# Sixteen modulation blocks as narrow products on TensorE, with the first group's loads, row squares and scales in another order

## The chip, the cores and the metric

The kernel runs on one core of a Trainium2 chip. The metric is the device time of one execution in microseconds; three runs of the kernel before took 1738.68, 1740.67 and 1740.92 us, median 1740.67. TensorE does the matrix products, VectorE (DVE) and ScalarE (ACT) the elementwise work, GpSimd (POOL) a few elementwise operations, and SyncE (SP) issues nearly all loads.

## The reference, cut to what matters

Two transformer blocks on 256 tokens of width 1024, in float32. The change touches only the start of the first block, where a condition vector makes shift and gain for a normalised input that is then projected:

```python
mod = silu(c) @ w_mod + b_mod               # 6 x 1024; and the same with c_ctx
h  = rms_norm(x,   norm1_g) * (1 + mod[1])   + mod[0]
hc = rms_norm(ctx, norm1_g) * (1 + mod_c[1]) + mod_c[0]
proj, projc = h @ w_in, hc @ w_in            # then retention and attention heads
# attention, w_out, PEER experts (16384), then a second block: FFN, gated MLP, SSM, FFN, gate
```

## The kernel before, in words

All large weights come from one array, `wall`, in chunks of 1024 KB (128 x 2048 float32), each made of two halves. They land in three buffers, `raw`. SP issues the load of chunk n when both halves of chunk n-3 have been read (`read(u)`, L548). A half of a projection weight is read by two operations: ACT rounds it to `w_hi` (L1410), and DVE or POOL writes the rest as `w_lo` (L1851 or L2602); TensorE then makes three products per tile from the pairs. Up to four such pairs are held, made ahead of use in the order that `REACH` sets.

The first ten chunks hold the 16 blocks of `w_mod` for shift (blocks 0 to 7) and gain (8 to 15), each 1024 x 128, and the four halves `win 0,0` to `win 0,3` of the first projection group. A "quarter" h is the four blocks 2h, 2h+1, 2h+8, 2h+9, which give shift and gain of the feature blocks 2h and 2h+1 for x and for ctx. One list, `front_steps` (L150), is walked by every engine, and each does its part of each step in that order:

- `mod n`: for n below 8, DVE multiplies the 128 x 1024 block by the condition row of ctx (L2010) and of x (L2013), each with a sum along the row. For n in `MOD_PE` (8 to 15) TensorE does it: eight products (sixteen in the trace, which shows a float32 product with few columns as two) with the block as the stationary operand and only two moving columns, c and c_ctx (`mod_block`, L888). These are the narrow products. From block 16 on, DVE does them with its own loads.
- `diag 0`, `diag 1`: scale of the rows of x and of ctx as diagonal matrices, from row squares made by ACT.
- `xturn h`, `cturn h`: TensorE transposes and scales two feature blocks of x, of ctx ("turns"). A turn waits until the one before it in the same bank has been read (`s_f`, `s_fh`).
- `gain h` (`gains`, L2019): DVE adds the bias and makes the gain from the four blocks of a quarter. `rows h`: DVE and ACT scale, shift and split the turned blocks into `HX` (x) and `HC` (ctx).
- `win 0,h`: TensorE's 12 products of 512 columns over `HX`. It waits for the two `HX` blocks of rows h and for the `w_lo` half.
- `evac 0`: ACT copies the finished projection out of the banks, which lets the next group (`win 1,0`) start. Behind it stand the squares and roots of `unit 0` and `unit 1`, with block 16 of `w_mod` between them.

Of the kernel before, what the change touches and what calls it, by code (L numbers as in the profile page):

```python
# [142 lines left out]

MOD_PE = list(range(8, 16))
NMOD = 16


def front_steps():  # L150


    steps = []

    def mods(*ns):
        steps.extend(("mod", n) for n in ns)

    def win(p, h, *more):
        steps.append(("win", p, h))
        steps.extend(more)  # L160

    mods(0, 8, 1, 9)
    steps.extend([("diag", 0), ("xturn", 0)])
    mods(2)
    steps.extend([("diag", 1), ("cturn", 0), ("gain", 0), ("rows", 0)])
    mods(10, 3, 11)
    steps.extend([("xturn", 1), ("cturn", 1), ("gain", 1), ("rows", 1)])
    win(0, 0)
    mods(12, 4, 13, 5)
    steps.extend([("xturn", 2), ("cturn", 2), ("gain", 2), ("rows", 2)])  # L170
    win(0, 1)
    mods(14, 6, 15, 7)
    steps.extend([("xturn", 3), ("cturn", 3), ("gain", 3), ("rows", 3)])
    win(0, 2)
    win(0, 3, ("evac", 0))
    win(1, 0, ("square", 0), ("square", 1), ("unit", 0))
    mods(16)
    win(1, 1, ("rope", 0), ("unit", 1))
    mods(17, 18)
    win(1, 2, ("rope", 1))  # L180
    mods(19, 20)
    win(1, 3, ("evac", 1), ("gammas", 0))
    mods(21)
    win(2, 0, ("square", 2), ("square", 3), ("unit", 2), ("qturn", 0), ("qturn", 1))
    mods(22)
    win(2, 1, ("rope", 2), ("unit", 3), ("qturn", 2), ("qturn", 3))
# [12 lines left out]
    steps.extend([("score", 2), ("weigh", 0), ("turn", 1)])
    win(4, 0, ("score", 3), ("weigh", 1), ("turn", 2))  # L200
    mods(30, 31)
    steps.extend([("score", 4), ("weigh", 2), ("turn", 3)])
    win(4, 1, ("score", 5), ("weigh", 3), ("turn", 4), ("rope", 4))
    mods(32, 33)
    win(4, 2, ("score", 6), ("weigh", 4), ("turn", 5), ("rope", 5))
    mods(34, 35)
    win(4, 3, ("evac", 4), ("score", 7), ("weigh", 5), ("turn", 6))
    mods(36, 37)
    mods(38, 39)
    steps.extend([("weigh", 6), ("turn", 7), ("rturn", 0)])  # L210
    win(5, 0, ("mask", 0), ("weigh", 7))
    win(5, 1, ("rturn", 1), ("mask", 1), ("madd", 0))
    win(5, 2, ("rscore", 0), ("mask", 2), ("dvar", 0), ("madd", 1))
    win(5, 3, ("added", 1), ("droot", 0), ("rscore", 1), ("evac", 5), ("madd", 2), ("dnorm", 0))
    steps.extend([("rweigh", 0), ("rscore", 2), ("mask", 3), ("rweigh", 1), ("dblocks", 0), ("madd", 3)])
    steps.extend([("out", 0), ("rscore", 3), ("out", 1), ("rweigh", 2), ("rweigh", 3), ("rnorm", 0)])
    steps.extend([("out", 2), ("out", 3)])
    return steps
# [7 lines left out]

SPLIT = [u for u in range(U_END) if u >= U_OUT1 or HALVES[u][0] == "win"]
ORD = {u: n for n, u in enumerate(SPLIT)}
LO_POOL |= {HALF_OF["win", p, h] for p in (0,) for h in range(4)}

GATE2 = range(40, 48)
MOD_V = [s[1] for s in FRONT if s[0] == "mod" and s[1] not in MOD_PE] + list(GATE2)
# [152 lines left out]
def program(nc, wall, keys_d, cols_d, rows_d, bigrows_d, crow_d, wmod_d, dist_d, x_d, ctx_d, pT_d, gws_d, out_d, n_chunks):  # L385
    assert n_chunks * 2 == U_END
    with ExitStack() as es:
# [413 lines left out]

        def sync_program(e):
            e.dma_start(cols[:, :], cols_d).then_inc(s_tab, 16)
            e.dma_start(crow_ctx, crow_d[1024:2048].partition_broadcast(128)).then_inc(s_crow, 16)
            e.dma_start(crow, crow_d[0:1024].partition_broadcast(128)).then_inc(s_crow, 16)
            for n in range(n_chunks):
                if n == 1:
                    e.dma_start(x[:, :, :], x_d.rearrange("(i p) d -> p i d", p=128)).then_inc(s_x, 16)
                if n == 2:
                    e.dma_start(ctx, ctx_d.rearrange("(i p) d -> p i d", p=128)).then_inc(s_ctx, 16)  # L810
                if n == 6:
                    e.dma_start(rows[:, :], rows_d.partition_broadcast(128)).then_inc(s_tab, 16)
                if n == 10:
                    e.wait_ge(s_tab, 32)
                    e.dma_start(dist, dist_d.rearrange("p (a b) -> p a b", a=4)).then_inc(s_tab, 16)
                if n == 11:
                    e.wait_ge(s_c2, 3)
                    e.dma_start(crow_keep.rearrange("(p d) -> p d", p=1), crow[0:1, :]).then_inc(s_ckeep, 16)
                if n == U_QUERY // 2:
                    e.wait_ge(s_pt_, 8)  # L820
# [7 lines left out]
                for m in MOD_ISSUE.get(n, []):  # L828
                    place, times = mod_slot(m)
                    if m < NMOD + 4:  # L830
                        e.wait_ge(*summed(7))
                        e.wait_ge(s_std, 2)
                    elif m == GATE2[0]:
                        e.wait_ge(s_w, 24)
                        e.wait_ge(s_ckeep, 16)
                        e.dma_start(crow2, crow_keep.partition_broadcast(128)).then_inc(s_rawm[4], 16)
                    else:
                        e.wait_ge(*summed(m - (1 if m in GATE2 else 4)))
                    e.dma_start(mod_raw[place], wmod_d[m - NMOD]).then_inc(s_rawm[place], 16)
# [26 lines left out]
        def tensor_program(e):  # L866
# [23 lines left out]
            def mod_block(n):  # L890
# [1 line left out]
                w = raw_half(u).rearrange("p (k n) -> p k n", k=8)  # L892
                t.wait_ge(*landed(u))
                t.wait_ge(s_c2, 1)
                quarter, q = n % 8 // 2, MOD_PE.index(n)
                if quarter >= 2:
                    t.wait_ge(s_mod, quarter - 1)
                for k in range(8):
# [501 lines left out]
        def scalar_program(e):  # L1400
# [109 lines left out]

            a.wait_ge(s_tab, 16)
            act(c2, c2, ACT.Silu, sig=s_c2)
            a.wait_ge(s_crow, 32)
            for r in (crow_ctx, crow):
                act(r, r, ACT.Silu, sig=s_c2)
            a.wait_ge(s_set, 1)
            for j, (src, here) in enumerate(((x, s_x), (ctx, s_ctx))):
                a.wait_ge(here, 16)
                for i in range(2):
                    act(scr, src[:, i, :], ACT.Square, scale=1.0 / 32, acc=rs[:, 2 * j + i:2 * j + i + 1])  # L1520
# [3 lines left out]
                return pj(n, 1536, 2048) if n < 2 else pj(n - 2, 2048, 2560)  # L1524

            for name, n, *more in FRONT:
                if name == "gammas":
                    softplus_parts(0, sa[:, 0:8], sb_[:, 0:8], sc[:, 0:8])
                    a.wait_ge(s_lam, 1)
                    act(sa[:, 0:2], sa[:, 0:2], ACT.Exp, sig=s_lama)  # L1530
                elif name == "rows":
                    for b in range(4 * n, 4 * n + 4):
                        high(b)
                    ahead(HALF_OF["win", 0, n], only=True)
                elif name == "win":
                    ahead(HALF_OF[(name, n, *more)])
                elif name == "evac":
                    g, u = GROUPS[n], HALF_OF["win", n, 3]
                    for i in tiles_of(g):
# [4 lines left out]
                            a.wait_ge(s_win, WIN_MADE[n, i])  # L1544
                        src = PB[2][:, 256 * (i == 2):256 + 256 * (i == 2)] if narrow else PB[i][:, :]
                        act(pj(i, g * 512 + 256 * narrow, (g + 1) * 512), src, ACT.Silu if g == 2 else ACT.Copy, sig=s_wev)
                elif name == "square":
                    if n >= 2:
                        a.wait_ge(s_qn, n - 1)
# [294 lines left out]
        def vector_program(e):  # L1844
# [29 lines left out]
                v.settle()  # L1874
                v.did(e.reciprocal(out, a_), sig)

            def ahead(u):

                nonlocal made
                while made < REACH[u]:  # L1880
                    w = SPLIT[made]
                    if w not in LO_POOL:
                        v.wait_ge(s_hi, made + 1)
# [111 lines left out]
            def mod_block(n):  # L1995


                c_ = crow
                if n >= NMOD:
                    place, times = mod_slot(n)  # L2000
                    w = mod_raw[place]
                    if n >= GATE2[0]:
                        times, c_ = times + 1, crow2
                    v.wait_ge(s_rawm[place], 16 * times + 16)
                else:
                    u = HALF_OF["mod", n]
                    w = raw_half(u)
                    v.wait_ge(*landed(u))
                    v.wait_ge(s_c2, 2)
                    v.did(e.scalar_tensor_tensor(junk, w, 1.0, crow_ctx, MUL, MUL, accum_out=modT[:, n, 1:2]))  # L2010
                    v.wait_ge(s_c2, 3)
                v.settle()
                v.did(e.scalar_tensor_tensor(w, w, 1.0, c_, MUL, MUL, accum_out=modT[:, n, 0:1]), s_modv)  # L2013

# [3 lines left out]

            def gains(h):  # L2019

                quarter = (2 * h, 2 * h + 1, 2 * h + 8, 2 * h + 9)
                v.wait_ge(s_modu, max(MOD_PE.index(n) for n in quarter if n in MOD_PE) + 1)
                for n in quarter:
                    src = modT[:, n, :]
                    if n in MOD_PE:
                        src = pm[h % 2][:, MOD_PE.index(n), :]
                    ts(modT[:, n, :], src, col("bmod")[:, n:n + 1], op0=ADD, sig=s_mod if n == 2 * h + 9 else None)
                s_ = slice(2 * h, 2 * h + 2)
                stt(G1[:, s_, :], modT[:, 2 * h + 8:2 * h + 10, :], 1.0, bc(col("n1")[:, s_], 2, 2), ADD, MUL)

# [57 lines left out]
            for name, n, *more in FRONT:  # L2088
# [21 lines left out]
                elif name == "rows":  # L2110
                    scaled(4 * n)
                    scaled(4 * n + 1)
                    for b in range(4 * n, 4 * n + 4):
                        low(b)
                elif name == "win" and (n, *more) != (5, 3):
                    ahead(HALF_OF[(name, n, *more)])
# [637 lines left out]
```

## Time and profile before

| | |
|---|---|
| median of three runs | 1740.67 us |
| profiled execution: span from the first to the last instruction | 1738.2 us |
| lowest and highest run | 1738.68 and 1740.92 us |
| PE, DVE, ACT busy | 1647.9, 1250.9, 907.9 us |
| the front, up to the first product of `win 1,0` | 71.38 us |

The profile gives the profiled execution its span; the time of that execution as a whole is not given apart from the three runs, whose lowest lies 0.5 us and whose median 2.5 us above the span. TensorE is busy 95% of the span, but in the front it is not: the change touches the first 4% of the span alone. A chain of waits is read from the end backwards; the timeline of an engine gives its groups of instructions in order of time, with the idle time before a group in brackets and what ended it. `ar` is the large work area (it holds ctx, the condition rows, the attention arrays), `pb` the accumulation banks, `raw` the chunks.

### The profile page before, as it was taken

The page shows a single profiled execution, that of the slowest core. Times are in us where ns is not written, and L with a number is a line of the kernel's source. Part 1 is how long each engine was busy: PE and PEld are TensorE (multiplying, and loading weights), DVE is VectorE, ACT ScalarE, POOL GpSimd, SP SyncE. Part 2 cuts the span into 40 slices and gives each one's busy share as a digit, 9 for nine tenths or more (in the row PEclk, how much of TensorE's full clock was granted, in tenths as well). Part 3 has the DMA queues.
Part 4 walks back from the last instruction along what each step waited for, and adds up shares of the span by engine and source line. Part 5 has one row for each costly group of instructions (what it writes and reads, how often), then busy time and mean ns, then how long its engine had stood idle before and what let it go on. Part 6 is the DMA issues. An engine that isn't in the chain of part 4 may idle for free.

```text
span 1738.2 us, 29000 instructions
## 1 busy us (share of the span) xinstructions
PE 1647.9 (95%) x11512; PEld 1479.5 (85%) x11512; DVE 1250.9 (72%) x2028; ACT 907.9 (52%) x1192; POOL 83.8 (5%) x50
## 2 busy tenths in 40 slices
PE   6898788999999999999999999999998989999997
PEld 6776668998999888789999999899998777899996
DVE  5886666899988899986666655655557787655556
ACT  4354555554555555455444445544446766644446
POOL 1100003522000000000000000000000000000000
PEclk9898999999999999999999999999999999999999
DMA  6644233446565455566555565454554533555551
GB/s 264 274 168 157 97 118 137 155 161 206 189 202 188 170 207 192 207 218 249 203 211 216 195 214 187 150 204 177 194 173 155 203 137 121 200 194 174 193 191 73
DMA packets 53418, 318.52 MB, mean 183 GB/s; under 512 B 5953, under 2 KB 6113, under 8 KB 19362
## 3 DMA queue, kind: packets, MB, share of 16 engines
q1 hardware_dynamic: 52098, 310.60, 50.2%
q0 software_dynamic: 1184, 6.05, 0.9%
q8 instruction: 91, 1.49, 0.3%
q14 instruction: 45, 0.37, 0.1%
HBM read 307.17 MB, written 9.47 MB: 182 GB/s over the span
## 4 chain that ended last, share of the span: by engine, by line
PE 73%; DVE 18%; ACT 6%; issue 1%; DMA 1%; SPq 0%; DVEq 0%; ACTq 0%
PE pb L870 73%; DVE w_lo L1851 4%; DVE ar L1851 4%; ACT ar L1410 3%; DVE ar L1863 2%; ACT w_hi L1410 2%; DVE ar L2215 1%; DMA raw<-in_wall 1%; DVE ar L2013 1%; DVE ar L2212 1%; DVE raw L2013 1%; ACT L1410 1%; DVE ar L2010 1%; DVE ar L2219 1%; DVE sm L2078 0%
## 5 line engine op out<-in xcount | busy, mean ns | idle before, releaser
L1851 DVE TENSOR_TENSOR w_lo<-raw,w_hi 128x1024 fp32r<-128x1024 f32 x467 | 572.2, 1225 | 253.2 <-ACT w_hi L1410 227.7
L870 PE MATMUL pb<-HX,w_hi 128*128 128x256 f32 x3904 | 715.8, 285 | 13.0 <-DVE w_lo L1851 6.0
L1410 ACT ACTIVATE w_hi<-raw 128x1024 fp32r<-128x1024 f32 x498 | 528.3, 1061 | 299.3 <-PE pb L870 278.3
L870 PEld LDWEIGHTS pb<-HX,w_hi 128*128 128x128 f32 x3904 | 613.8, 193 | 20.1 <-DVE w_lo L1851 5.2
L870 PE MATMUL pb<-HX,w_lo 128*128 128x256 f32 x1952 | 553.7, 284 | 0.0
L870 PE MATMUL pb<-w_hi,HC 128*128 128x512 f32 (+1 forms) x1648 | 526.3, 391 | 4.2 <-DVE HC L1863 3.3
L870 PEld LDWEIGHTS pb<-HX,w_lo 128*128 128x128 f32 x1952 | 376.0, 193 | 0.0
L870 PEld LDWEIGHTS pb<-w_hi,HC 128*128 128x128 f32 x1648 | 309.6, 188 | 68.6 <-DVE HC L1863 2.7
L870 PE MATMUL pb<-w_lo,HC 128*128 128x512 f32 (+1 forms) x824 | 320.6, 389 | 0.0
L1851 DVE TENSOR_TENSOR ar<-ar 128x512 bf16<-128x512 bf16 (+8 forms) x470 | 247.7, 564 | 53.2 <-ACT ar L1410 33.5
L1410 ACT ACTIVATE ar<-pb 128x512 f32<-128x512 f32 (+3 forms) x200 | 112.4, 562 | 256.5 <-PE pb L870 155.4
L870 PE MATMUL pb<-w_hi,HX 128*128 128x512 f32 x512 | 175.2, 409 | 10.6 <-DVE HX L1851 4.2
L870 PEld LDWEIGHTS pb<-w_lo,HC 128*128 128x128 f32 x824 | 155.3, 188 | 28.9
L870 PE MATMUL pb<-ar 128*128 128x64 bf16 (+3 forms) x1960 | 127.9, 224 | 19.1 <-ACT ar L1410 8.8
L870 PEld LDWEIGHTS pb<-ar 128*128 128x128 bf16 (+2 forms) x1960 | 106.5, 121 | 42.4 <-issue 22.6
L870 PEld LDWEIGHTS pb<-w_hi,HX 128*128 128x128 f32 x512 | 99.7, 195 | 36.9 <-issue 7.9
L1410 ACT ACTIVATE HC<-ar 128x512 fp32r<-128x512 f32 x87 | 55.0, 633 | 93.4 <-PE pb L870 52.1
L870 PE MATMUL pb<-w_lo,HX 128*128 128x512 f32 x256 | 102.3, 400 | 0.0
L1851 DVE TENSOR_TENSOR HC<-ar,HC 128x512 fp32r<-128x512 f32 x87 | 60.3, 693 | 45.0 <-ACT HC L1410 41.3
L2602 POOL TENSOR_TENSOR w_lo<-raw,w_hi 128x1024 fp32r<-128x1024 f32 x31 | 75.8, 2444 | 151.1 <-ACT w_hi L1410 110.9
L1410 ACT ACTIVATE ar<-ar 128x512 f32<-128x512 f32 (+6 forms) x85 | 50.2, 591 | 52.5 <-DVE ar L1858 18.0
L870 PEld LDWEIGHTS pb<-w_lo,HX 128*128 128x128 f32 x256 | 50.1, 196 | 9.2
(148 smaller groups left out, 705.5 us busy)
## 6 DMA issues: line engine op xcount, KB each, us to landing
raw<-in_wall SPq DMA_DIRECT2D x257, 1024.0 KB, 4.8
ar<-in_wmod SPq DMA_DIRECT2D x24, 512.0 KB, 3.7
act_keep<-ar SPq DMA_DIRECT2D x28, 256.0 KB, 5.6
ar<-act_keep SPq DMA_DIRECT2D x28, 256.0 KB, 5.1
x<-in_wmod SPq DMA_DIRECT2D x8, 512.0 KB, 5.3
ar<-in_bigrows POOLq DMA_DIRECT2D x2, 1024.0 KB, 5.3
ar<-acs_keep POOLq DMA_DIRECT2D x2, 1024.0 KB, 8.2
ar<-in_crow SPq DMA_DIRECT2D x2, 512.0 KB, 6.0
```

Source lines behind the costliest of these rows:

```text
L870: return e.matmul(o, l, r, start=start, stop=stop, skip_group_check=True)
L1410: a.did(e.activation(out, in_, func, scale=scale, **kw), sig)
L1851: v.did(e.tensor_tensor(out, a_, b_, op), sig)
L1863: v.did(e.scalar_tensor_tensor(out, a_, s_, b_, op0, op1), sig)
L2010: v.did(e.scalar_tensor_tensor(junk, w, 1.0, crow_ctx, MUL, MUL, accum_out=modT[:, n, 1:2]))
L2013: v.did(e.scalar_tensor_tensor(w, w, 1.0, c_, MUL, MUL, accum_out=modT[:, n, 0:1]), s_modv)
L2212: v.did(e.max(vals[:, c_], src))
L2215: v.did(e.max_index(idx[:, c_], vals[:, c_], src))
L2219: v.did(e.match_replace(src, vals[:, c_], src, NEG))
L2602: p.did(e.tensor_tensor(w_lo[:, made % NH, :], raw_half(w), w_hi[:, made % NH, :].bitcast(F32), SUB), s_lop)
```

## The change

`MOD_PE` holds all sixteen blocks, ordered by quarters. DVE no longer does a block below 16. The whole of quarter 0 now stands ahead of `diag 0`, and `cturn h` stands behind `gain h`; `xturn h+1` stands ahead of `win 0,h`. The row squares move into the step `diag`. The broadcast load of the ctx condition row is gone and that of c (512 KB) moves from the head of the queue to chunk 8; its silu moves behind `evac 0`. The bias of a quarter is added by one operation in place of four. The `w_lo` halves of `win 0,0` to `win 0,3` go from POOL to DVE, and in `rows h` the `win 0,h` half stands ahead of the two ctx blocks.

```diff
-MOD_PE = list(range(8, 16))
+MOD_PE = [0, 8, 1, 9, 2, 10, 3, 11, 4, 12, 5, 13, 6, 14, 7, 15]
...
-    mods(0, 8, 1, 9)
+    def quarter(h):
+        mods(*MOD_PE[4 * h:4 * h + 4])
+
+    quarter(0)
     steps.extend([("diag", 0), ("xturn", 0)])
-    mods(2)
-    steps.extend([("diag", 1), ("cturn", 0), ("gain", 0), ("rows", 0)])
-    mods(10, 3, 11)
-    steps.extend([("xturn", 1), ("cturn", 1), ("gain", 1), ("rows", 1)])
+    quarter(1)
+    steps.extend([("gain", 0), ("diag", 1), ("cturn", 0), ("rows", 0), ("xturn", 1)])
     win(0, 0)
...
+    quarter(3)
+    steps.extend([("gain", 2), ("cturn", 2), ("rows", 2), ("xturn", 3)])
     win(0, 2)
+    steps.extend([("gain", 3), ("cturn", 3), ("rows", 3)])
     win(0, 3, ("evac", 0))
...
-LO_POOL |= {HALF_OF["win", p, h] for p in (0,) for h in range(4)}
...
-            e.dma_start(crow_ctx, crow_d[1024:2048].partition_broadcast(128)).then_inc(s_crow, 16)
-            e.dma_start(crow, crow_d[0:1024].partition_broadcast(128)).then_inc(s_crow, 16)
...
+                if n == 8:
+                    e.dma_start(crow, crow_d[0:1024].partition_broadcast(128)).then_inc(s_crow, 16)
...
                 elif name == "rows":
-                    for b in range(4 * n, 4 * n + 4):
+                    for b in (4 * n, 4 * n + 1):
                         high(b)
                     ahead(HALF_OF["win", 0, n], only=True)
+                    for b in (4 * n + 2, 4 * n + 3):
+                        high(b)
...
+                    if n == 0:
+                        a.wait_ge(s_crow, 16)
+                        act(crow, crow, ACT.Silu, sig=s_c2)
...
-                for n in quarter:
-                    src = modT[:, n, :]
-                    if n in MOD_PE:
-                        src = pm[h % 2][:, MOD_PE.index(n), :]
-                    ts(modT[:, n, :], src, col("bmod")[:, n:n + 1], op0=ADD, sig=s_mod if n == 2 * h + 9 else None)
+                v.wait_ge(s_modu, 4 * h + 4)
+                pair = slice(2 * h, 2 * h + 2)
+                tt(modT[:, 0:16, :].rearrange("p (s k) j -> p s k j", s=2)[:, :, pair, :],
+                   pm[h % 2][:, h // 2 * 4:h // 2 * 4 + 4, :].rearrange("p (s k) j -> p s k j", s=2),
+                   bc(col("bmod")[:, 0:16].rearrange("p (s k) -> p s k", s=2)[:, :, pair], 3, 2), ADD, sig=s_mod)
```

The start of TensorE's program before: `cols,raw` are narrow products (eight to a block), `ar,x` is a turn of x, `ar` alone a turn of ctx, `w_hi,HX` and `w_lo,HX` a projection half.

```order
L870 MATMUL pb<-cols,raw 128x2 x16
L870 MATMUL pb<-ar,x 128x128 x4
L870 MATMUL pb<-ar 128x128 x4
L870 MATMUL pb<-cols,raw 128x2 x16
L870 MATMUL pb<-ar,x 128x128 x4
L870 MATMUL pb<-ar 128x128 x4
L870 MATMUL pb<-w_hi,HX 128x512
```

The same place with the change:

```order
L870 MATMUL pb<-cols,raw 128x2 x32
L870 MATMUL pb<-ar,x 128x128 x4
L870 MATMUL pb<-cols,raw 128x2 x32
L870 MATMUL pb<-ar 128x128 x4
L870 MATMUL pb<-ar,x 128x128 x4
L870 MATMUL pb<-w_hi,HX 128x512
```

Two blocks between turns have become four, in every quarter; the first two quarters stand ahead of `win 0,0` with one turn between them.

DVE's program from the scaling of rows 2 to that of rows 3, before (`fsc<-pb` and `HX` are the x blocks, `HC` the ctx blocks, L2010 and L2013 the row products of a block of `w_mod`, `modT` and `sm` the gain):

```order
L1858 TENSOR_SCALAR fsc<-pb,sm,modT 128x256 x2
L1851 TENSOR_TENSOR HX<-fsc,HX 128x256 x2
L1851 TENSOR_TENSOR HC<-fsc,HC 128x256 x2
L2010 SCALAR_TENSOR_TENSOR ar,modT<-raw,ar 128x1024
L2013 SCALAR_TENSOR_TENSOR raw,modT<-raw,ar 128x1024
L2010 SCALAR_TENSOR_TENSOR ar,modT<-raw,ar 128x1024
L2013 SCALAR_TENSOR_TENSOR raw,modT<-raw,ar 128x1024
L1856 TENSOR_SCALAR modT<-modT,cols 128x2 x2
L1856 TENSOR_SCALAR modT<-pb,cols 128x2 x2
L1863 SCALAR_TENSOR_TENSOR sm<-modT,cols 128x4
L1858 TENSOR_SCALAR fsc<-pb,sm,modT 128x256 x2
```

The same place with the change:

```order
L1863 TENSOR_SCALAR fsc<-pb,sm,modT 128x256 x2
L1856 TENSOR_TENSOR HX<-fsc,HX 128x256 x2
L1856 TENSOR_TENSOR HC<-fsc,HC 128x256 x2
L1856 TENSOR_TENSOR w_lo<-raw,w_hi 128x1024 x2
L1856 TENSOR_TENSOR modT<-pb,cols 128x2x4
L1868 SCALAR_TENSOR_TENSOR sm<-modT,cols 128x4
L1863 TENSOR_SCALAR fsc<-pb,sm,modT 128x256 x2
```

The four row products are gone from between the two, and two `w_lo` halves of group 1 have come from behind rows 3 to ahead of `gain 3`.

ACT's program around `evac 0` (`ar<-pb` copies the banks out, `ar<-ar 128x1024` is the silu of the condition row, `ar<-ar 128x512` the squares, `ar<-ar 128x8` the root), as a difference:

```order
+L1410 ACTIVATE w_hi<-raw 128x1024
 L1410 ACTIVATE ar<-pb 128x512 x2
+L1410 ACT_TABLE_LOAD
+L1410 ACTIVATE ar<-ar 128x1024
 L1410 ACTIVATE w_hi<-raw 128x1024
 L1410 ACTIVATE ar<-ar 128x512 x2
+L1410 ACT_TABLE_LOAD
 L1410 ACTIVATE ar<-ar 128x8
```

A silu with its table, and the table of the root again, now stand between the copies out of the banks and the root of `unit 0`.

## Rows read from the trace of the kernel before

**Rows 1.** The chain of waits, 0 to 160 us: start, us, what.
```profile
57.26 3.32 DVE ar L2010 x2
...
71.38 22.07 PE pb L870 x96
```
**Rows 2.** Groups by line, 0 to 71.3 us: busy, mean ns, idle before.
```profile
L870 PE MATMUL pb<-cols,raw 128*128 128x2 f32 x128 | 21.2, 300 | 12.1 <-DMA raw<-in_wall 12.1
L2013 DVE SCALAR_TENSOR_TENSOR raw<-raw,ar 128x1024 f32<-128x1024 f32 x8 | 15.9, 1982 | 0.3
...
L2010 DVE SCALAR_TENSOR_TENSOR ar<-raw,ar 128x1024 f32<-128x1024 f32 x8 | 11.9, 1490 | 14.7 <-DMA raw<-in_wall 14.7
```
**Rows 3.** Timeline of PE in the front: start, us, idle before.
```profile
10.65 3.58 PE L870 MATMUL pb<-cols,raw 128*128 128x2 f32 x16 [10.65 <-DMA raw<-in_wall]
15.69 3.58 PE L870 MATMUL pb<-cols,raw 128*128 128x2 f32 x16 [1.47 <-DMA raw<-in_wall]
...
26.10 6.83 PE L870 MATMUL pb<-cols,raw 128*128 128x2 f32 x32
32.79 2.05 PE L870 MATMUL pb<-ar,x 128*128 128x128 f32 x8
...
36.20 0.70 PE L870 MATMUL pb<-w_hi,HX 128*128 128x512 f32 x1
...
39.27 3.63 PE L870 MATMUL pb<-cols,raw 128*128 128x2 f32 x32
42.76 1.39 PE L870 MATMUL pb<-ar,x 128*128 128x128 f32 x8
...
45.51 0.77 PE L870 MATMUL pb<-w_hi,HX 128*128 128x512 f32 x1
...
48.99 3.63 PE L870 MATMUL pb<-cols,raw 128*128 128x2 f32 x32
52.47 1.14 PE L870 MATMUL pb<-ar,x 128*128 128x128 f32 x8
...
65.42 0.77 PE L870 MATMUL pb<-w_hi,HX 128*128 128x512 f32 x1 [4.17 <-DVE HX L1851]
...
70.25 0.63 PE L870 MATMUL pb<-w_hi,HX 128*128 128x512 f32 x1
```
**Rows 4.** Stretches of 1 us; the column after POOL is the granted clock.
```profile
43.00:44.00 1.00, 1.00 (x9) 1.00 (x9) 1.00 (x1) 0.00 (x0) 0.23 (x1) 0.75 0.92 385
...
53.00:54.00 1.00, 1.00 (x10) 1.00 (x9) 0.97 (x2) 0.97 (x2) 0.40 (x1) 0.87 0.42 164
```
**Rows 5.** Timeline of ACT at the start and around `evac 0`.
```profile
4.04 0.22 ACT L1410 ACTIVATE cols<-cols 128x16 f32<-128x16 f32 x1 [1.96 <-DMA cols<-in_cols]
...
64.93 0.56 ACT L1410 ACTIVATE fsc<-pb,modT,sm 128x256 f32<-128x256 f32 x1
...
67.17 3.38 ACT L1410 ACTIVATE w_hi<-raw 128x1024 fp32r<-128x1024 f32 x3
70.64 1.29 ACT L1410 ACTIVATE ar<-pb 128x512 f32<-128x512 f32 x2
...
94.15 1.28 ACT L1410 ACT_TABLE_LOAD   x1
```
**Rows 6.** Timeline of DVE in and behind the front.
```profile
63.25 1.12 DVE L1858 TENSOR_SCALAR fsc<-pb,sm,modT 128x256 f32<-128x256 f32 x2
...
74.41 0.69 DVE L1871 TENSOR_REDUCE ar<-ar 128x8 f32<-128x512 f32 x1
...
95.69 0.17 DVE L1856 TENSOR_SCALAR sm<-sm 128x8 f32<-128x8 f32 x1 [0.71 <-ACT sm L1410]
97.27 0.38 DVE L1856 TENSOR_SCALAR sm<-sm 128x8 f32<-128x8 f32 x2 [1.41 <-ACT sm L1410]
```
**Rows 7.** Loads, 0 to 110 us: KB each, median us from issue to landing.
```profile
raw<-in_wall SPq DMA_DIRECT2D x17, 1024.0 KB, 5.6
```
**Rows 8.** The page's group of the `w_lo` halves on DVE.
```profile
L1851 DVE TENSOR_TENSOR w_lo<-raw,w_hi 128x1024 fp32r<-128x1024 f32 x467 | 572.2, 1225 | 253.2 <-ACT w_hi L1410 227.7
```

More of the change, by code:

```diff
@@ L160, in win @@
         steps.extend(more)
-    mods(0, 8, 1, 9)
+    def quarter(h):
+        mods(*MOD_PE[4 * h:4 * h + 4])
+    quarter(0)
     steps.extend([("diag", 0), ("xturn", 0)])
-    mods(2)
-    steps.extend([("diag", 1), ("cturn", 0), ("gain", 0), ("rows", 0)])
-    mods(10, 3, 11)
-    steps.extend([("xturn", 1), ("cturn", 1), ("gain", 1), ("rows", 1)])
+    quarter(1)
+    steps.extend([("gain", 0), ("diag", 1), ("cturn", 0), ("rows", 0), ("xturn", 1)])
     win(0, 0)
-    mods(12, 4, 13, 5)
-    steps.extend([("xturn", 2), ("cturn", 2), ("gain", 2), ("rows", 2)])
+    quarter(2)
+    steps.extend([("gain", 1), ("cturn", 1), ("rows", 1), ("xturn", 2)])
     win(0, 1)
-    mods(14, 6, 15, 7)
-    steps.extend([("xturn", 3), ("cturn", 3), ("gain", 3), ("rows", 3)])
+    quarter(3)
+    steps.extend([("gain", 2), ("cturn", 2), ("rows", 2), ("xturn", 3)])
     win(0, 2)
+    steps.extend([("gain", 3), ("cturn", 3), ("rows", 3)])
     win(0, 3, ("evac", 0))
@@ L569, in program @@
         assert a2.at <= 2048
-        crow_ctx, scr, junk = msk[:, 0, :], msk[:, 1, :], msk[:, 2, :]
+        scr = msk[:, 1, :]
         def pj(i, a, b):
@@ L808, in sync_program @@
                     e.dma_start(x[:, :, :], x_d.rearrange("(i p) d -> p i d", p=128)).then_inc(s_x, 16)
-                if n == 2:
+                if n == 3:
                     e.dma_start(ctx, ctx_d.rearrange("(i p) d -> p i d", p=128)).then_inc(s_ctx, 16)
-                if n == 6:
+                if n == 8:
+                    e.dma_start(crow, crow_d[0:1024].partition_broadcast(128)).then_inc(s_crow, 16)
+                if n == 9:
                     e.dma_start(rows[:, :], rows_d.partition_broadcast(128)).then_inc(s_tab, 16)
@@ L815, in sync_program @@
                     e.dma_start(dist, dist_d.rearrange("p (a b) -> p a b", a=4)).then_inc(s_tab, 16)
-                if n == 11:
-                    e.wait_ge(s_c2, 3)
+                if n == U_OUT1 // 2 - 1:
+                    e.wait_ge(s_c2, 2)
                     e.dma_start(crow_keep.rearrange("(p d) -> p d", p=1), crow[0:1, :]).then_inc(s_ckeep, 16)
@@ L830, in sync_program @@
                     if m < NMOD + 4:
-                        e.wait_ge(*summed(7))
                         e.wait_ge(s_std, 2)
@@ L894, in mod_block @@
                 t.wait_ge(s_c2, 1)
-                quarter, q = n % 8 // 2, MOD_PE.index(n)
+                quarter, q = n % 8 // 2, 4 * (n % 8 // 4) + n // 8 * 2 + n % 2
                 if quarter >= 2:
@@ L1512, in scalar_program, with row_squares @@
             act(c2, c2, ACT.Silu, sig=s_c2)
-            a.wait_ge(s_crow, 32)
-            for r in (crow_ctx, crow):
-                act(r, r, ACT.Silu, sig=s_c2)
             a.wait_ge(s_set, 1)
-            for j, (src, here) in enumerate(((x, s_x), (ctx, s_ctx))):
+            def row_squares(j, src, here):
                 a.wait_ge(here, 16)
@@ L1526, in scalar_program @@
             for name, n, *more in FRONT:
-                if name == "gammas":
+                if name == "diag":
+                    row_squares(n, *((ctx, s_ctx) if n else (x, s_x)))
+                elif name == "gammas":
                     softplus_parts(0, sa[:, 0:8], sb_[:, 0:8], sc[:, 0:8])
@@ L1875, in rcp, with ahead @@
                 v.did(e.reciprocal(out, a_), sig)
-            def ahead(u):
+            def ahead(u, only=False):
                 nonlocal made
-                while made < REACH[u]:
+                while made < (ORD[u] + 1 if only else REACH[u]):
                     w = SPLIT[made]
@@ L1998, in mod_block @@
                 c_ = crow
[L1999 to L2004, printed above, removed]
-                else:
-                    u = HALF_OF["mod", n]
-                    w = raw_half(u)
-                    v.wait_ge(*landed(u))
+                place, times = mod_slot(n)
+                w = mod_raw[place]
+                if n >= GATE2[0]:
+                    times, c_ = times + 1, crow2
+                else:
                     v.wait_ge(s_c2, 2)
-                    v.did(e.scalar_tensor_tensor(junk, w, 1.0, crow_ctx, MUL, MUL, accum_out=modT[:, n, 1:2]))
-                    v.wait_ge(s_c2, 3)
+                v.wait_ge(s_rawm[place], 16 * times + 16)
                 v.settle()
@@ L2019, in gains @@
             def gains(h):
-                quarter = (2 * h, 2 * h + 1, 2 * h + 8, 2 * h + 9)
-                v.wait_ge(s_modu, max(MOD_PE.index(n) for n in quarter if n in MOD_PE) + 1)
-                for n in quarter:
-                    src = modT[:, n, :]
-                    if n in MOD_PE:
-                        src = pm[h % 2][:, MOD_PE.index(n), :]
-                    ts(modT[:, n, :], src, col("bmod")[:, n:n + 1], op0=ADD, sig=s_mod if n == 2 * h + 9 else None)
+                v.wait_ge(s_modu, 4 * h + 4)
[3 more added lines that the diff above has]
+                   bc(col("bmod")[:, 0:16].rearrange("p (s k) -> p s k", s=2)[:, :, pair], 3, 2), ADD, sig=s_mod)
                 s_ = slice(2 * h, 2 * h + 2)
@@ L2112, in vector_program @@
                     scaled(4 * n + 1)
-                    for b in range(4 * n, 4 * n + 4):
+                    for b in (4 * n, 4 * n + 1):
+                        low(b)
+                    ahead(HALF_OF["win", 0, n], only=True)
+                    for b in (4 * n + 2, 4 * n + 3):
                         low(b)
```

## The prediction, as made before the changed kernel ran

> **What bounds the kernel now.** I read the chain of waits first, then the groups of the first 71 us, then the timelines of TensorE, ScalarE and VectorE. The reader is to see in the chain that the front hangs on the row products of `w_mod` blocks on VectorE and the small operations that follow them, and from 71.38 us TensorE with 22 us of projection without a break [rows 1]. Before them stand the first loads, for which TensorE waits 12.1 us [rows 2]. In the groups, the 16 row products on VectorE take 15.9 + 11.9 = 27.8 us (means 1.98 and 1.49 us). TensorE's eight narrow blocks take 21.2 us [rows 2]. So VectorE is the bound of the front and TensorE has gaps, the last 4.17 us before `win 0,3` [rows 3]. Everything behind 71.38 us hangs on that point: no load or engine runs to a clock of its own. The effect of the change is the shift of that restart, plus what is new just behind it.
>
> **TensorE's two speeds.** This decides. The same two narrow blocks take 6.83 us at 26.10 and 3.63 at 39.27 [rows 3]. The granted clock reads 1.00 over the first 43 us, so there I go by durations; from 43 us both agree: it falls to half (1.2 GHz) at about 43.5 and 53.7 from 2.4 GHz [rows 4]. Start to start, a block costs (32.79 - 26.10)/2 = 3.35 us at the low clock, 3.54 from 15.69; I take 3.4. At the high clock (42.76 - 39.27)/2 = 1.75. A turn costs (36.20 - 32.79)/2 = 1.7 low and at most 1.14 high (at 52.47) [rows 3]; I take 1.0. What comes before each change is regular: with narrow products alone the clock never rose, though TensorE worked on them from 26.10 to 32.79; turns and a projection half raised it. It fell 43.5 - 39.27 = 4.2 us and 53.7 - 48.99 = 4.7 us after a row of narrow products had begun, each time when they were already over, so the two blocks were still fast and the turns behind them slow.
>
> **The change part by part, along TensorE.**
>
> *Start.* The two condition loads of 512 KB leave the head of the queue. `cols` is there at 4.04 and the first chunk at 10.65 [rows 3, 5]: 6.6 us for 2048 KB, of which 1024 remain: 3.3 us, so the first chunk lands at 7.35 (bounds 6.5, at the pace of 5.0 us for x and a chunk, 10.65 to 15.69, and 8.5).
>
> *Quarter 0.* Four blocks at 3.4 = 13.6: done at 20.95. Chunk 1 (two loads behind the first, 5.0 us) is there at 12.4 and is not waited for. Row squares and scales of x are done by then, since ctx and x come no later than before.
>
> *Turn 0, quarter 1.* 1.7, then 13.6 at the low clock: 36.25. Chunk 3 is asked for when chunk 0 has been read, at 14.2, and comes behind the queue at about 20; it is needed at 29.5. Later chunks take 5.6 us from the request [rows 7], and each request comes a quarter or more ahead of its use. Loads bound nothing from 7.35 on.
>
> *Turns and `win 0,0`.* Two turns 3.4: 39.65. The clock rises about here, as it did before `win 0,0`, which takes 39.27 - 36.20 = 3.07 [rows 3]: 42.7. Its `HX` blocks and its half are ready 15 us earlier.
>
> *Quarter 2.* Four blocks from the high clock. It falls some 4.5 us after they begin: 4.5/1.75 = 2.6 blocks fast, 1.4 slow at 3.4 = 4.8. Together 9.3: 52.0.
>
> *Turns, `win 0,1`, quarter 3, turns, `win 0,2`.* 3.4 (slow), 48.99 - 45.51 = 3.5, 9.3, 3.4, 3.5: 75.1. The last turn at the high clock, 1.0: 76.1.
>
> *`win 0,3`.* Its `HX` blocks are now late for a new reason. ctx turn 2 ends at 71.6 - 1.7 = 69.9. Then ACT makes the ctx blocks of rows 2, 67.17 - 64.93 = 2.2 [rows 5]: 72.1; then two `w_hi` halves at 3.38/3 = 1.13: 74.4; VectorE's second `w_lo`, which stands ahead of `gain 3`, 1.2 [rows 8]: 75.6; gain 0.4 (an estimate: two small operations in place of five); scaling and splitting the two x blocks 65.42 - 63.25 = 2.2 [rows 3, 6]: 78.2. TensorE waits 2.1 us in place of 4.17. With 3.0 for the half it ends at 81.2, and by the lead of before (the first half of group 1 begins when ACT has copied a bank out, 71.38 [rows 1] against a `win 0,3` that ends at 70.9 [rows 3]) group 1 begins at 81.6 (ACT itself, with 2.2 for the ctx blocks and 1.1 for one more `w_hi`, gets there no later). Against 71.38: **+10.2 us**.
>
> *Behind `evac 0`.* A table load 1.28 [rows 5] and a silu of 128 x 1024, which has the shape of a `w_hi` at 1.1 [rows 5], stand ahead of the squares: VectorE's `unit 0` is 2.4 us later. The second table load lies in VectorE's reduction but for 0.3. VectorE then works nearly without a break to 95 us, where it waits 0.71 and 1.41 us for ACT [rows 6]; the first of these swallows 0.7, the second recurs, as it is ACT's own table change. **+1.9 us** (bounds 0, if VectorE is not what the later chain hangs on, and 3.7, all three operations in full).
>
> *Nothing.* VectorE's 27.8 us [rows 2] go from the path, but VectorE would then wait for TensorE; its four `w_lo` halves and the three bias additions less per quarter lie under TensorE's quarters. The condition row is needed by block 16 at the earliest and lands 30 us before.
>
> *Sum.* 10.2 + 1.9 = 12.1 us. On the profiled span 1738.2: 1750.3. The median of the runs lies 2.5 us above that span, so the forecast is 1740.7 + 12.1 = **1752.8 us**, 0.7% slower. The trade in one line: TensorE takes eight blocks more, 8 x 1.75 = 14 us at best and 8 x 3.4 = 27 at worst, plus slower turns, and has only 3.3 us of earlier start and the gaps of before to put them in.
>
> **A rule of the Trainium skill.** With narrow products only, from 26.10 to 32.79 and from 10.65 on, the rate stayed at the low clock [rows 3]. The page "TensorE: Matmul & The Clock Gate", section "Why this matters for your kernels", says that TensorE should be kept busy continuously to come to the full clock. By that rule the unbroken quarters 0 and 1 would raise it; the trace here does not agree, as the 6.7 us without a break show. What would follow if it did rise is rival C.
>
> **Rivals.**
>
> *A, the low clock throughout the front.* Longer narrow rows never let it up. A half then costs 5.1 (`win 0,3` before, 65.42 to 70.9, shows 5.5). From 39.65: 5.2, 13.6, 3.4, 5.2, 13.6, 3.4, 5.2, 1.7, 5.2 = 96.2; restart 96.7, +25.3, with 1.9: 1768. For it: `win 0,3` ran low from end to end. Against: two turns and a half raised the clock twice, and they still stand in a row.
>
> *B, the high clock stays once it is up.* From 42.7: quarter 7.0, turns 2.0, half 3.1, quarter 7.0: ctx turn 2 ends at 62.8, `HX` 8.3 later at 71.1, half 3.1: restart 74.7, +3.3, with 1.9: 1746. Against: it fell twice in shorter narrow rows [rows 4].
>
> *C, the other side: the clock rises inside quarter 0 or 1.* Unlike before, TensorE has no gap after 12 us. Quarter 1 and all behind at the high clock: 20.95 + 1.0 + 7.0 + 2.0 + 3.1 = 34.1, + 7.0 + 2.0 + 3.1 + 7.0 = 53.2, ctx turn 2 at 54.2, `HX` at 62.5, restart at 66.1: -5.3, with 1.9 it is -3.4: 1737. It decides from a narrow block of 1.75 us before the first turn of ctx; taking VectorE off the path then wins. Against: 26.10 to 32.79.
>
> **How the numbers follow.** Forecast 0.75 (clock as before in its manner, 1746 to 1760 by the bounds of start, clock phase of up to a half, 2.3 us, and the unit term), A 0.08, B 0.10, C 0.07. The range from 1746 to 1764 holds the forecast's cases and half of B, and leaves A and C out. A measurement of this kernel can tell about 0.2%, 3.5 us: faster is the larger part of C, 0.05; the same 0.05, from the rest of C and the low end of B; slower 0.90.
>
> **What would show each step.** First narrow product near 7.35. Quarters 0 and 1 at 13.6 us each. A granted clock of 0.5 over the end of quarters 2 and 3 and the turns behind them, with quarters of 9 to 10 us. A wait of about 2 us on `HX` ahead of `win 0,3`. The first product of group 1 near 81.6. VectorE's first reduction of `unit 0` 6.2 us behind ACT's first copy (74.41 - 70.64 = 3.8 before [rows 5, 6]), and no other stretch changed. Wrong if quarter 1 runs in 7 us, or if TensorE waits for `raw` loads after 12 us.

## The result, and the profile after

| | before | after |
|---|---|---|
| median of the runs (4 each, same chip) | 1739.68 us | 1752.45 us |
| lowest and highest | 1738.25 and 1740.92 | 1750.86 and 1754.91 |
| profiled execution, span | 1738.2 | 1749.1 |
| PE, DVE, ACT busy | 1647.9, 1250.9, 907.9 | 1670.3, 1225.2, 909.2 |
| first product of `win 1,0` | 71.38 | 83.88 |

The ratio is 1.0075, with 95% interval 1.0061 to 1.0089: 12.8 us slower in medians, 10.9 in the two profiled spans (the profiled execution of after is the fastest of its four, 1750.86). The forecast was 1752.8.

The busy times already tell the trade: VectorE works 25.7 us less, TensorE 22.4 us more. The stretch up to the first product of group 1 (`win 1,0`) shows where; that of after ends 0.2 us behind it. Columns: stretch, length, busy time and instructions of PE, PEld, DVE, ACT and POOL, granted clock, DMA share, GB/s. First before, then after.

```profile
0.00:71.40 71.40, 50.51 (x241) 45.67 (x241) 46.93 (x85) 29.35 (x48) 11.17 (x9) 0.88 0.71 277
```
```profile
0.00:84.10 84.10, 73.92 (x369) 71.11 (x370) 22.16 (x45) 27.16 (x46) 0.30 (x5) 0.86 0.66 252
```

TensorE had 21 us of gaps in its front and now has 10, of which 7.46 are the first load. The chain of waits of after (start, us, what) has TensorE alone from 7.46 to 70.8 where that of before had VectorE's row products [rows 1]:

```profile
1.25 6.16 DMA raw<-in_wall
7.46 63.37 PE pb L870 x328
73.08 1.07 ACT w_hi L1410
74.17 1.24 DVE w_lo L1856
75.50 1.24 DVE w_lo L1856
77.30 0.56 DVE fsc L1863
79.48 4.59 PE pb L870 x12
84.09 0.61 ACT ar L1410
```

TensorE's timeline of after (start, us, idle before), to be laid against [rows 3]:

```profile
7.46 13.82 PE L870 MATMUL pb<-cols,raw 128*128 128x2 f32 x64 [7.46 <-DMA raw<-in_wall]
21.14 2.06 PE L870 MATMUL pb<-ar,x 128*128 128x128 f32 x8
22.99 13.65 PE L870 MATMUL pb<-cols,raw 128*128 128x2 f32 x64
36.50 2.06 PE L870 MATMUL pb<-ar 128*128 128x128 f32 x8
...
39.72 0.49 PE L870 MATMUL pb<-w_hi,HX 128*128 128x512 f32 x1
...
42.58 10.22 PE L870 MATMUL pb<-cols,raw 128*128 128x2 f32 x64
52.67 2.06 PE L870 MATMUL pb<-ar 128*128 128x128 f32 x8
...
56.08 0.71 PE L870 MATMUL pb<-w_hi,HX 128*128 128x512 f32 x1
...
59.14 9.76 PE L870 MATMUL pb<-cols,raw 128*128 128x2 f32 x64
...
72.17 0.77 PE L870 MATMUL pb<-w_hi,HX 128*128 128x512 f32 x1
...
75.71 1.05 PE L870 MATMUL pb<-ar 128*128 128x128 f32 x8
79.48 0.47 PE L870 MATMUL pb<-w_hi,HX 128*128 128x512 f32 x1 [2.71 <-DVE HX L1856]
...
83.45 0.82 PE L870 MATMUL pb<-w_hi,HX 128*128 128x512 f32 x2
84.12 0.39 PE L870 MATMUL pb<-w_lo,HX 128*128 128x512 f32 x1
```

The row at 83.45 holds the twelfth and last product of `win 0,3`, which ends at 84.07, and the first of group 1, which starts at 83.88. The 84.09 at the end of the chain is ACT's second copy out of the banks, not TensorE.

Quarters 0 and 1 run at 3.4 us a block from end to end. Quarters 2 and 3 begin fast and end slow. Stretches of 1 us of after give the points (the clock is the number behind POOL's): it falls at 46.3, 3.7 us into quarter 2, and at 63.4, 4.3 us into quarter 3. It falls once more behind the last turn:

```profile
46.00:47.00 1.00, 1.00 (x8) 1.00 (x8) 0.43 (x1) 0.00 (x1) 0.00 (x0) 0.67 0.59 246
...
63.00:64.00 1.00, 1.00 (x8) 1.00 (x9) 0.85 (x3) 0.71 (x2) 0.00 (x0) 0.70 0.40 66
...
80.00:81.00 1.00, 1.00 (x5) 0.81 (x4) 0.43 (x1) 0.88 (x3) 0.00 (x0) 0.73 1.06 430
...
83.00:84.00 1.00, 1.00 (x4) 0.79 (x3) 0.84 (x1) 0.27 (x1) 0.00 (x0) 0.56 0.26 107
```

That last fall, 1 us into `win 0,3` and right behind a wait of 2.71 us, makes this half cost 4.6 us from its start to its end. Behind it, VectorE's first reduction of `unit 0` moved from 74.41 [rows 6] to 89.59, and TensorE's first product behind it (L937) from 128.59 to 143.28. The chains from there, first before, then after:

```profile
128.59 1.78 PE pb L937 x8
130.36 5.11 PE pb L870 x24
135.47 0.45 PE pb L937 x4
...
234.35 13.03 PE pb L870 x64
278.04 54.03 PE pb L870 x440
```
```profile
143.28 1.09 PE pb L937 x8
144.37 4.17 PE pb L870 x24
148.54 0.45 PE pb L937 x4
...
247.47 13.04 PE pb L870 x64
291.24 54.03 PE pb L870 x440
```

The row of 64 products, called "the x64" from here on, serves as a later mark. The shift is 14.7 us at L937 x8, 13.1 in the third row, and then stays: 13.1 at the x64, 13.2 at the x440, 13.3 at 1020 us. What goes in between is clock: the same 32 products took 6.89 us before (granted clock 0.50 from 129 to 132 us) and 5.26 after (1.00 from 144 to 147). Late in the span the shift falls to 12.5 (1316 us) and, where 64 products took 11.79 us before and 10.14 after, to 10.6 (1459 us). The code there is untouched.

### The profile page after: what moved, and what is told of

The parts are those of the page before. It is cut to its first block, busy times and chain, and to the rows that moved or that the text cites. A ratio compares the mean times of both kernels' runs of the same rounds, so it can differ in the third digit from the quotient of the medians.

```text
span 1749.1 us, 29206 instructions
## 1 busy us (share of the span) xinstructions
PE 1670.3 (95%) x11640; PEld 1504.6 (86%) x11640; DVE 1225.2 (70%) x1988; ACT 909.2 (52%) x1193; POOL 73.2 (4%) x46
## 4 chain that ended last, share of the span: by engine, by line
PE 75%; DVE 17%; ACT 6%; issue 1%; DMA 0%; DVEq 0%; ACTq 0%; SPq 0%
PE pb L870 74%; DVE w_lo L1856 4%; DVE ar L1856 4%; ACT ar L1410 3%; DVE ar L1868 2%; ACT w_hi L1410 2%; DVE ar L2012 1%; DVE ar L2215 1%; DVE ar L2212 1%; ACT L1410 1%; DVE ar L2219 1%; DVE sm L2075 0%; ACT HX L1410 0%; DMA raw<-in_wall 0%; DVE ar L1861 0%
## 5 line engine op out<-in xcount | busy, mean ns | idle before, releaser
L1410 ACT ACTIVATE ar<-ar 128x512 f32<-128x512 f32 (+8 forms) x84 | 49.2, 586 | 49.3 <-DVE ar L1863 17.8
L2602 POOL TENSOR_TENSOR w_lo<-raw,w_hi 128x1024 fp32r<-128x1024 f32 x27 | 64.8, 2401 | 104.0 <-ACT w_hi L1410 63.2
```

The source lines that it names most:

```text
L1410: a.did(e.activation(out, in_, func, scale=scale, **kw), sig)
L2602: p.did(e.tensor_tensor(w_lo[:, made % NH, :], raw_half(w), w_hi[:, made % NH, :].bitcast(F32), SUB), s_lop)
```

## The experiments

Two theories of the 12.8 us were open. **T**: TensorE's own narrow work at the low clock is the cost; waits and the silu are small change. **W**: the new order of the elementwise work (the wait on `HX`, the silu, the halves on VectorE) costs most of it, and sixteen narrow blocks as such would pay. `before` ran in each session: medians 1739.59, 1739.06, 1739.41.

**Silu early.** After, with the silu of the condition row in the step `win 0,1`.

```diff
                     ahead(HALF_OF[(name, n, *more)])
+                    if (n, *more) == (0, 1):
+                        a.wait_ge(s_crow, 16)
+                        act(crow, crow, ACT.Silu, sig=s_c2)
...
-                    if n == 0:
-                        a.wait_ge(s_crow, 16)
-                        act(crow, crow, ACT.Silu, sig=s_c2)
```

> The changed kernel with the silu of the condition row moved ahead of evac 0, into ACT's idle stretch behind the halves of win 0,1; nothing else. Theory (the front's length is TensorE's, and the silu with its table stands on the path behind evac 0): TensorE's front unchanged, unit 0's first reduction 2.3 us nearer to ACT's first copy, TensorE's first use of group 2's result (the first product of line 937 after 128 us) 2 us earlier, whole kernel about 2 us shorter than the change, 1750.5. Rival (VectorE is not what the later chain hangs on there): the reduction moves by 2.3 us, the later point and the whole time by 0.3 or less.

Measured: 1750.76 us (1750.27 to 1751.16, 4 runs), ratio to before 1.0068 (1.0051 to 1.0085). L937 comes at 140.69 in place of 143.28, of which 0.3 is an earlier first load, so the term of about 2.3 us is real at this point. But the next 24 products now run at the low clock, 5.75 us for 4.17, and the x64 comes at 247.09 (247.47), no more than the 0.3 of the start earlier. The term does not reach the later stages: the profiled spans are 1749.2 and 1749.1 us. The median is 1.7 us below that of after, near the 2 expected, but the two sets of runs overlap and can't tell it.

**Halves of group 1 later.** After, with the `w_hi` and `w_lo` halves that stood ahead of rows 3 put behind them.

```diff
-                    ahead(HALF_OF[(name, n, *more)])
+                    ahead(HALF_OF[(name, n, *more)], only=(n, *more) == (0, 2))
```

> The changed kernel with the two high and low halves of group 1 made behind rows 3 and no longer ahead of them. Theory (win 0,3 is late since ACT and VectorE first make two halves of group 1): the wait of 2.7 us on HX ahead of win 0,3 goes, win 0,3 runs at the high clock in 2.8 us where it took 4.6, but ACT then has three w_hi to make before it copies the banks out, so group 1 starts only about 1 us earlier (83.0 against 84.1). Rival (the turns and the gain set win 0,3, not the halves): the wait stays above 2 us and group 1 starts where it did or later.

Measured: 1750.67 us (1749.19 to 1751.23, 4 runs), ratio 1.0069 (1.0053 to 1.0086). The wait on `HX` is gone, but one on ACT takes its place, since ACT makes three `w_hi` ahead of its copies. TensorE's timeline of this run:

```profile
81.95 0.77 PE L870 MATMUL pb<-w_hi,HX 128*128 128x512 f32 x1 [3.41 <-ACT ar L1410]
```

`win 0,3` begins without a wait and takes 3.0 us where it took 4.6, at the high clock. Group 1 begins 1.9 us earlier than after's 83.88, 0.5 of it the earlier first load (6.92), and the x64 comes at 245.27, 2.2 earlier. The wait and the slow half behind it account for about 2 of the 12.8 us, not for most of them. This run alone can't say more, since a new wait stands in the place of the old one.

**Dense products beside the narrow ones.** After, with 512-column float32 products into an unused bank: four ahead of the first block and k behind each block of quarters 0 and 1, k = 1 and k = 2.

```diff
+def dense(k):
+    for _ in range(k):
+        mm(PB[0][:, :], ident, cols[:, NCOL - 512:NCOL], True, True)
```

> The changed kernel with extra TensorE work whose results are not used: four products of 512 float32 columns ahead of block 0 while the first chunk is on its way, and one behind each block of quarters 0 and 1. Clock theory (the narrow blocks cost 3.4 us because the clock stays low over them, and dense products raise it): if one dense product per block is enough, the narrow blocks of quarters 0 and 1 take 1.75 us each, and the two quarters with their extra products about 11 us each. If it is not enough they stay at 3.4 and each quarter takes 20 us. Rival (3.4 us is what sixteen weight loads of a cold buffer or loads from HBM beside them cost, whatever the clock): 3.4 us each also where the granted clock is high.

> As warm1 with two dense products behind each block of quarters 0 and 1. Clock theory: the narrow blocks of quarters 0 and 1 take 1.75 us each, each quarter with its eight extra products 14 to 15 us, so the start of win 0,0 stays within 2 us of where it was though TensorE does 20 products more. Rival (the rate of the narrow products has nothing to do with the clock): 3.4 us each and the two quarters together 40 us, win 0,0 13 us later.

Measured (one run each): 1761.21 us with one, 1755.86 with two. With one, the first two blocks of quarter 0 take 1.84 us, the next 2.46 and 3.41, and in quarter 1 1.98, 2.58, 3.41, 3.41. With two, all eight take 1.84. The granted clock goes with it. With one, it reads 1.00 from 11 to 16 us, 0.50 from 18 to 27, 1.00 from 28 to 30 and 0.50 from 32 to 47; with two, it reads 1.00 from 8.5 to 45. TensorE's timeline with two, start and end of that stretch:

```profile
4.49 5.50 PE L870 MATMUL pb<-cols 128*128 128x512 f32 x8 [4.49 <-DMA cols<-in_cols]
9.83 1.84 PE L870 MATMUL pb<-cols,raw 128*128 128x2 f32 x16
11.54 1.96 PE L870 MATMUL pb<-cols 128*128 128x512 f32 x4
...
35.25 1.84 PE L870 MATMUL pb<-cols,raw 128*128 128x2 f32 x16
```

So the 3.4 us are the clock. They are not the stationary side, which is the same in fast and slow blocks, and not the loads: with one dense product the DMA share is 0.98 from 11 to 16 us, beside the fast blocks, and 0.39 from 18 to 27, beside the slow ones. Narrow products do not hold the clock up here; two dense ones behind each block do, and one does not. Twenty dense products more, and `win 0,0` begins at 40.45 us in place of 39.72: up to there they nearly pay for themselves. Behind it they do not: quarter 2 takes 11.33 us from start to start (10.09 in after), group 1 begins at 85.39, and the one run is 3.4 us above after's median.

**Six blocks back on VectorE.** After, with blocks 2 to 7 as row products again (the condition rows loaded at chunk 2, their silus behind x's squares); a second kernel does this with blocks 4 to 7 alone (rows at chunk 4, silus at `gain 0`).

```diff
-MOD_PE = [0, 8, 1, 9, 2, 10, 3, 11, 4, 12, 5, 13, 6, 14, 7, 15]
+MOD_ALL = [0, 8, 1, 9, 2, 10, 3, 11, 4, 12, 5, 13, 6, 14, 7, 15]
+MOD_PE = [n for n in MOD_ALL if n not in [2, 3, 4, 5, 6, 7]]
```

> The changed kernel with blocks 4 to 7 (the shift blocks of quarters 2 and 3) back on VectorE, and both condition rows loaded behind ctx, their silus in ACT's idle stretch of quarter 1. Theory (TensorE is the bound of the front with the change, and VectorE has some 8 us free in each quarter): quarters 2 and 3 take 3.5 us each on TensorE in place of 10, group 1 starts at 67 to 70 us (84.1 with the change, 71.4 before), whole kernel 1737 to 1740, that is 13 us below the change and level with or just below the kernel before. Rival (VectorE's row products become the bound again, as before): group 1 starts at 72 or later and the time is above that of the kernel before.

> As mix12, and blocks 2 and 3 on VectorE too: quarter 0 all on TensorE, the others split in halves as in the kernel before; condition rows loaded behind chunk 1. Theory: quarter 1 takes 7 us on TensorE in place of 13.5, and group 1 starts at 62 to 68 us: 1731 to 1737. Rival (VectorE is the bound from here on, and gets the blocks in front of gain and rows): no earlier than mix12.

Measured: 1751.25 us with four blocks back (1750.65 to 1753.83, 4 runs, ratio 1.0077, 1.0059 to 1.0094) and 1743.18 with six (1741.4 to 1747.25, 10 runs, 1.0025, 1.0015 to 1.0035). Both are slower than before, where 1737 to 1740 and 1731 to 1737 were expected. Quarters 2 and 3 fall to 3.5 us each, as expected, but most of it turns into a wait. Four blocks back, TensorE's timeline:

```profile
55.44 3.63 PE L873 MATMUL pb<-cols,raw 128*128 128x2 f32 x32
...
68.43 2.07 PE L873 MATMUL pb<-ar,x 128*128 128x128 f32 x8 [8.36 <-DVE fsc L1867]
```

and VectorE's at the same place:

```profile
59.10 2.56 DVE L1860 TENSOR_TENSOR w_lo<-raw,w_hi 128x1024 fp32r<-128x1024 f32 x2 [6.28 <-ACT w_hi L1413]
```

VectorE's row products stand behind two `w_lo` halves, and these wait for a `w_hi` whose chunk ACT itself waited 5.7 us for. The group start that I expected at 67 to 70 us came at 81.42: the order of the halves is a second bound that the narrow products had covered. *Both bounds off* below tests this. With six blocks back, quarter 1 falls to 6.7 us, but group 1 begins at 74.43 in place of 62 to 68, behind a wait at the same place:

```profile
60.68 2.08 PE L873 MATMUL pb<-ar,x 128*128 128x128 f32 x8 [7.57 <-DVE fsc L1867]
```

**POOL's halves.** Before, with nothing changed but its four `w_lo` halves, which go from POOL to VectorE.

```diff
-LO_POOL |= {HALF_OF["win", p, h] for p in (0,) for h in range(4)}
```

> The kernel before with one part of the change alone: the w_lo halves of win 0,0 to 0,3 on VectorE in place of POOL. My view (VectorE's row products are slowed while POOL works beside them: 27.8 us for 16, against 19.6 at 1.22 each): VectorE loses the 8 us of slowing and gains four halves at 1.23, so its chain in the front gets 3 us shorter, 1737 us. Rival (the halves stand in the way of the next quarter on VectorE, and the slowing lay beside waits): the same as before or 2 to 5 us longer.

Measured: 1743.79 us (1741.6 to 1745.25, 10 runs), ratio 1.0023 (1.0013 to 1.0032). My view was wrong in sign. The row products beside POOL are indeed faster, all 1.22 to 1.23 us; in before four of sixteen took 3.24 to 3.38, each while POOL worked. One of the four, in VectorE's and POOL's timelines of before:

```profile
29.69 1.22 DVE L2010 SCALAR_TENSOR_TENSOR ar<-raw,ar 128x1024 f32<-128x1024 f32 x1
...
30.95 3.24 DVE L2013 SCALAR_TENSOR_TENSOR raw<-raw,ar 128x1024 f32<-128x1024 f32 x1
```
```profile
30.55 2.57 POOL L2602 TENSOR_TENSOR w_lo<-raw,w_hi 128x1024 fp32r<-128x1024 f32 x1 [29.65 <-ACT w_hi L1410]
```

But VectorE then stands 4.31 us in front of a half whose `w_hi` isn't there, with the row products queued behind it; TensorE waits 4.01 us at 41.47 and 5.23 at 71.98, and group 1 begins at 77.94, 6.6 us late, of which 1.0 is a later first load in this run. The rival written down beside my view (the halves stand in the way of the next quarter, 2 to 5 us longer) is what happened.

**Both bounds off.** Six blocks back on VectorE, and in the front each engine makes only the half of its own quarter in rows h; of group 1, one half ahead of the copies of `evac 0` and the others behind.

```diff
-                while made < (ORD[u] + 1 if only else REACH[u]):
+                while made < (ORD[u] + int(only) if only else REACH[u]):
...
-                    ahead(HALF_OF[(name, n, *more)])
+                    ahead(HALF_OF[(name, n, *more)], only=n == 0)
                 elif name == "evac":
+                    if n == 0:
+                        ahead(HALF_OF["win", 0, 3], only=2)
```

> mix10 with one thing more: in the front each engine makes the halves of win 0,h only in rows h, and those of group 1 only at evac 0 (one ahead of the copies out of the banks, three behind), so that neither ACT nor VectorE stands before a chunk that has not landed while row products and scales could be made. Theory (mix10 lost its gain to that order: VectorE stood 5.3 us for the high half of win 0,2, and TensorE 7.6 us for the scales of x behind it): those two waits fall below 2 us each, group 1 starts at 64 to 68 us, whole kernel 1732 to 1737, faster than the kernel before. Rival (the chunk itself is late, whatever the order: three buffers and 5 to 9 us of landing bound the front): the waits only change their names, group 1 starts at 71 or later, 1740 or more.

Measured: **1735.31 us** (1733.85 to 1737.19, 10 runs), ratio to before 0.998 (0.997 to 0.9989): faster than both kernels, as expected, with group 1 at 65.17 us. No wait of TensorE in the front behind the first load is over 1.5 us:

```profile
7.01 13.81 PE L873 MATMUL pb<-cols,raw 128*128 128x2 f32 x64 [7.01 <-DMA raw<-in_wall]
...
43.52 0.50 PE L873 MATMUL pb<-w_hi,HX 128*128 128x512 f32 x1 [1.50 <-DVE w_lo L1864]
...
51.92 2.08 PE L873 MATMUL pb<-ar,x 128*128 128x128 f32 x8 [0.93 <-DVE fsc L1871]
...
65.17 0.50 PE L873 MATMUL pb<-w_hi,HX 128*128 128x512 f32 x1 [1.21 <-DVE w_lo L1864]
```

Of the 6.2 us by which group 1 begins earlier than in before, 3.6 are the earlier first load (7.01 for 10.65). Against before, this kernel differs in the split, the order of the loads and the order of the halves together; no run tells what each of them is worth.

**All sixteen, with the waits off.** After, with the late halves of the kernel above and the silu early: what is left of the loss when only the narrow products are.

> The changed kernel (all sixteen blocks on TensorE) with the same late halves and with the silu of the condition row in ACT's idle stretch. Theory (with the waits gone, TensorE's own work at its two clocks is all that is left of the front): no wait on HX or on a bank above 1.5 us, group 1 starts at 80 to 81 us (84.1 with the change, 71.4 before), whole kernel 1747 to 1750, still slower than before. Rival (the waits, not the narrow blocks, made the change slow): within 0.2% of the kernel before.

Measured: 1752.28 us (1750.83 to 1752.86, 4 runs), ratio 1.0071 (1.0056 to 1.0087). The waits are gone (0.94 and 0.65 us are left), and still group 1 begins late:

```profile
81.02 0.50 PE L870 MATMUL pb<-w_hi,HX 128*128 128x512 f32 x1 [0.65 <-DVE w_lo L1860]
```

Group 1 begins 2.9 us earlier than in after, 0.7 of it an earlier first load (6.79). At the x64 (246.94) 0.5 are left, no more than the earlier load, and none in the median, against the 1747 to 1750 expected. The kernel above (**Both bounds off**) ran on the same chip and differs by six blocks and the place of the silus: group 1 at 65.17 and 1735.31 us. That is 15.9 us of front and 17.0 us of time, though TensorE waits 3 us longer there. Per block it is 2.6 us, between the 1.75 and 3.4 of a block at either clock. **T** stands, **W** falls.

How much of it is the low clock, and how much only eight blocks more, can be estimated from rows. From start to start the sixteen blocks of after take 13.68 + 13.51 + 10.09 + 9.62 = 46.9 us, the eight of before are busy 21.2 [rows 2]. Of the 25.7 us between them, 8 x 1.75 = 14 would be there at the high clock too, and 11.7 are the low one, an estimate. No run shows all sixteen at the high clock without dense products between them.

## Why the prediction was right

*Start, quarters 0 and 1, turns.* First product 7.46 us (7.35 forecast), quarters 13.68 and 13.51 start to start (13.6), a turn 1.85 (1.7), two turns 3.22 (3.4). `win 0,0` begins at 39.72; the forecast had 39.65. Rival C, the clock rising in a long narrow row, would have shown a 1.75-us block before that point; there is none, and the dense products show what it takes. Unbroken narrow products of 13.7 us left the clock low. The Trainium skill, page "TensorE: Matmul & The Clock Gate", section "Why this matters for your kernels", would have had it up by then; this trace does not agree. The kind of product counts here, not only that the engine is never idle.

*`win 0,0` to the last turn.* 2.86, 10.09, 3.41, 3.06, 9.62, 3.41, 3.54 us, against 3.07, 9.3, 3.4, 3.5, 9.3, 3.4, 3.5: 36.0 for 35.5. The clock's manner (down in the narrow row, up again in the turns and the half) was as read from before; quarter 2 was 0.8 us dearer because it fell 3.7 us in, not 4.5. Rival A would have had halves of 5.2 us, rival B quarters of 7.0.

*`win 0,3`.* The chain that I gave, ACT's `w_hi`, the second `w_lo`, gain, scaling, is the one in the chain of after; its wait is 2.71 us for 2.1. The mis-sized term is the half behind it: 3.0 forecast, 4.6 measured, since the clock fell 1.0 us into it, behind the wait. Where the wait was gone (halves of group 1 later) it took 3.0. Before had shown the same thing, a half of 5.5 us behind a wait of 4.17 [rows 3], and I used it for rival A alone. The front comes out at +12.5 us for +10.2. The 2.3 us too little are 0.6 up to the last turn, 0.7 in that turn and the wait, and 1.6 in the half, less 0.6: I had group 1 start 0.4 us behind the end of `win 0,3`, as before, but ACT's first copy was done at 83.27 and TensorE went on without a wait.

*Behind `evac 0`.* VectorE's reduction stands 6.9 us behind ACT's first copy (6.2 forecast), its two idle times are 0.28 and 1.41 us, and L937 is 2.2 us later than the front explains (1.9). This term was right where I priced it, but it does not last: 1.6 us of it go at once to a clock that is high where before it was low, and the early silu shows the reverse, 2.3 us won and nothing kept. At the x64 0.6 us of it is left, and moving the silu wins next to nothing there (0.1 us beyond the earlier load).

*Sum.* 12.1 forecast, 13.1 to 13.3 from 148 to 1020 us, 10.9 at the end of this one pair of traces, 12.8 in the medians. The nearness of 1752.8 to 1752.45 is luck in part. The front was 2.3 us dearer than forecast, and what stands behind it 1.1 to 1.3 us cheaper up to 1020 us. The forecast was also added to 1740.7, the median of three runs, where that of four is 1739.68. The sign, the place and the mechanism are shown, the last microsecond is not. Why the untouched code runs 2 us shorter late in the profiled pair was not settled; the traces show that it goes with the clock, and not alike in each execution. With all sixteen blocks and the waits off, the same 64 products took 10.17 us, but the twelve products of a half behind them ran at the low clock (0.50 from 1470 to 1473 us) and took 1.6 us longer than in after.

*"Nothing".* VectorE's four halves of `win 0,h` cost nothing in the change, because TensorE covered them. In before itself the same move costs 4 to 5 us: the claim held under its condition only.

## What to carry to other kernels

A product with few columns is priced at the clock that a row of its own kind leaves behind (here 3.4 us a block, not the 1.75 that a short row shows), so work moved to TensorE in that form has to fit into its gaps at the dear price. Dense products put in for the clock alone won nothing in the whole kernel. Where two engines can do the same blocks, try a split: six of sixteen on VectorE gave the version that beats both, but only with the halves made later (1735.31 us); the split alone gave 1743.18. When a bound is taken away, look at what an engine holds in front of the newly critical instruction: here halves made ahead of use, each waiting for a chunk that had not landed.

## What was not expected of the hardware

A VectorE row product of 128 x 1024 took 3.24 to 3.38 us beside a POOL operation on tiles of the same size and 1.22 us otherwise; taking POOL's halves out removed all four long ones. The clock couples stages that share no data: in the early-silu run L937 came 2.6 us earlier, the 24 products behind it met the low clock, and 1.6 us of it were lost again (5.75 us for 4.17).
